# Sixteen modulation rows on TensorE as rows of PSUM instead of columns, in a two-block transformer kernel

## The reference, cut to what matters

```
c_act = silu(c)                                  # c: 1 x 1024
mod = c_act @ mod_w[l] + mod_b[l]                # 1 x 6144
sh1, sc1, g1, sh2, sc2, g2 = split(mod, 6)       # 1024 each
h = rmsnorm(x, norm_g[l, 0]) * (1 + sc1) + sh1
y = gla_mixer(h, ...)                            # gated linear attention
x = x + g1 * y
```

## Time and profile before

| | us |
|---|---|
| median of 3 runs | 2828.66 |
| lowest and highest of them | 2826.82, 2834.25 |
| profiled execution | 2830.2 |
| its span in the profile | 2828.1 |
| PE busy | 2742.2 (97%) |
| DVE busy | 2151.8 (76%) |
| ACT busy | 1324.3 (47%) |
| POOL busy | 1295.6 (46%) |

### The profile page before, as it was taken

The page is one execution under the profiler, slowest core; times in us unless marked ns, Lnnn a source line. Parts: engine busy times, 40 slices in busy tenths (PEclk is TensorE's granted clock), DMA queues, the critical chain, the costliest instruction groups (busy, mean ns, idle before and its releaser), DMA issues.

```text
span 2828.1 us, 53480 instructions
## 1 busy us (share of the span) xinstructions
PE 2742.2 (97%) x16662; PEld 2411.2 (85%) x16662; DVE 2151.8 (76%) x4127; ACT 1324.3 (47%) x2533; POOL 1295.6 (46%) x977
## 2 busy tenths in 40 slices
PE   6999999999999999899999999999999999999998
PEld 6688999999778877799999998777778989776666
DVE  7736996999888886758957898888867545467775
ACT  1115555333455555555564334555554633355553
POOL 4930897666444440006986664544420000244442
PEclk8999999999999999899999999999999999999999
DMA  7634555666666663144554566766635533389994
GB/s 257 214 115 134 183 181 194 203 204 207 236 238 233 229 227 115 42 159 149 184 173 141 174 202 211 260 222 230 223 141 170 177 131 122 111 327 359 356 356 167
DMA packets 179366, 562.52 MB, mean 199 GB/s; under 512 B 16288, under 2 KB 19104, under 8 KB 179120
## 3 DMA queue, kind: packets, MB, share of 16 engines
q1 hardware_dynamic: 176880, 556.86, 57.1%
q10 hardware_dynamic: 2368, 4.19, 0.4%
HBM read 559.94 MB, written 1.05 MB: 198 GB/s over the span
## 4 chain that ended last, share of the span: by engine, by line
PE 78%; PEld 6%; issue 6%; DVE 5%; POOL 2%; ACT 2%; DMA 1%; ACTq 0%; DVEq 0%; PEldq 0%; SPq 0%; POOLq 0%
PE bank L1113 22%; PE bank L1082 20%; PE bank L826 8%; PE bank L1406 7%; PEld bank L1082 6%; PE bank L1427 4%; PE bank L1062 4%; PE bank L885 4%; PE bank L850 1%; POOL arena L2902 1%; DVE h_parts L2435 1%; PE bank L771 1%; DVE a_parts L2438 1%; ACT arena L1702 1%; PE bank L1252 1%
## 5 line engine op out<-in xcount | busy, mean ns | idle before, releaser
L2848 POOL TENSOR_TENSOR w_parts<-ring,w_parts 128x512 fp32r<-128x512 f32 x512 | 667.2, 1310 | 511.5 <-ACT w_parts L1619 479.3
L1082 PE MATMUL bank<-h_parts,w_parts 128*128 128x256 f32 x6144 | 771.4, 285 | 4.4 <-POOL w_parts L2848 2.2
L1082 PEld LDWEIGHTS bank<-h_parts,w_parts 128*128 128x128 f32 x6144 | 747.5, 192 | 4.8 <-POOL w_parts L2848 2.4
L1619 ACT ACTIVATE w_parts<-ring 128x512 fp32r<-128x512 f32 x512 | 322.8, 631 | 436.3 <-PE bank L1082 435.8
L1113 PE MATMUL bank<-w_parts,a_parts 128*128 128x512 f32 x1536 | 370.3, 397 | 4.1 <-DVE a_parts L2438 4.1
L1113 PE MATMUL bank<-h_parts,a_parts 128*128 128x512 f32 x1536 | 365.7, 393 | 4.6 <-DVE a_parts L2438 4.4
L1113 PEld LDWEIGHTS bank<-h_parts,a_parts 128*128 128x128 f32 x1536 | 284.6, 188 | 79.1 <-DVE a_parts L2438 20.9
L1113 PEld LDWEIGHTS bank<-w_parts,a_parts 128*128 128x128 f32 x1536 | 286.0, 190 | 63.7 <-DVE a_parts L2438 5.1
L826 PE MATMUL bank<-h_parts,w_parts 128*128 128x256 f32 x2304 | 283.2, 285 | 4.0 <-DVE w_parts L2009 4.0
L826 PEld LDWEIGHTS bank<-h_parts,w_parts 128*128 128x128 f32 x2304 | 280.3, 193 | 5.1 <-issue 4.4
L1677 ACT ACTIVATE a_parts<-arena 128x256 fp32r (+1 forms) x256 | 107.0, 418 | 359.4 <-PE bank L1113 359.4
(11 more groups left out here) (397 smaller groups left out, 4318.1 us busy)
## 6 DMA issues: line engine op xcount, KB each, us to landing
ring<-stream SPq DMA_DIRECT2D x594, 512.0 KB, 3.3
arena<-stream SPq DMA_DIRECT2D x105, 1024.0 KB, 7.2
arena<-stream SPq DMA_DIRECT2D x144, 512.0 KB, 4.5
hT<-stream SPq DMA_DIRECT2D x96, 256.0 KB, 3.1
hT<-stream SPq DMA_DIRECT2D x32, 512.0 KB, 4.5
mean<-stream SPq DMA_DIRECT2D x32, 512.0 KB, 4.5
arena<-consts ACTq DMA_DIRECT2D x1, 1536.0 KB, 6.2
xT<-xin ACTq DMA_DIRECT2D x1, 1024.0 KB, 10.7
```

The source lines that it names most:

```text
L1082: mm = pe.matmul(bank[k][:, 0:T], w[:, wp, ws], h_parts[:, hp, 4 * j + q, :], start=(j == 0 and q == 0 and i == 0), stop=(j == 1 and q == ...
L1619: act.activation(w_parts[half % HALVES][:, 0, :], ring[slot_][:, j * 512:(j + 1) * 512], ACT.Copy).then_inc(sem(f"{n}_high"), 1)
L2848: pool.tensor_tensor(w[:, 1, :], ring[(base + k) % RING][:, j * 512:(j + 1) * 512], w[:, 0, :].bitcast(F32), ALU.subtract).then_inc(sem(f" ...
```

## The change

- Twelve rows are direct instead of seven, and DVE keeps four (2, 5, 8 and 11).
- In a direct row the operands change places. The column of `cact` is the stationary operand (128 x 1), the weights are the moving one (128 x 128), and eight matmuls add up in one row of PSUM: partition 0, 128 columns. Four rows share a bank; banks 4 and 5 are used in turn.
- ACT copies these rows from PSUM to partition 0 of a buffer in SBUF in four pieces (`first_rows_act`), and PE turns each row of 1 x 128 into a column of 128 x 1 by a matmul with a single one (`turned`): four behind the square sums, eight at the end. PE's rows 8 and 11 wait for earlier pieces to be copied.
- DVE's four rows no longer pass through the ring. Each has a buffer of its own into which it is loaded and in which it is multiplied.
- The ring holds 12 places for this stage instead of 16.
- The loads for POOL's rows 16 to 39 are issued later: the first behind place `gla` + 3 of the ring (whose load waits for the twelfth direct row), 18 in all spaced by four thirds of a place, and the last six behind `gla` + 27 as before.

```
-DIRECT_MODS = (0, 2, 4, 7, 9, 11, 13)
-SUMMED_MODS = tuple(m for m in range(FIRST_MODS) if m not in DIRECT_MODS)
+SUMMED_MODS = (2, 5, 8, 11)
+DIRECT_MODS = tuple(m for m in range(FIRST_MODS) if m not in SUMMED_MODS)
+N_DIRECT = len(DIRECT_MODS)
...
+        def first_row(i):
+            return G.v.rearrange("p a n -> p (a n)")[0:1, i * P:(i + 1) * P]
+        def first_bank(i):
+            return bank[(4, 5, 4)[i // 4] if i < 11 else 5]
...
-                if RING <= i < RING + FIRST_MODS:
-                    m = i - RING
-                    if m in DIRECT_MODS:
-                        sp.wait_ge(sem("first_direct"), DIRECT_MODS.index(m) + 1)
-                    else:
-                        sp.wait_ge(sem("first_product"), SUMMED_MODS.index(m) + 1)
+                if RING <= i < RING + N_DIRECT:
+                    sp.wait_ge(sem("first_direct"), i - RING + 1)
...
-            at = [8, 10, 14, gla + 1] + [gla + 2 + 3 * i // 2 for i in range(14)] + [gla + 27] * 6
-            loads_with_mods(0, MO["peer0_q"][1], MODS_GLA, MODS_GLA[0], at)
+            at = [gla + 3 + 4 * i // 3 for i in range(18)] + [gla + 27] * 6
+            for m in range(FIRST_MODS):
+                if m in SUMMED_MODS:
+                    i = SUMMED_MODS.index(m)
+                    sp.dma_start(first_buffer(i), stream[m]).then_inc(sem(f"first_landed{i}"), 16)
+                else:
+                    load(DIRECT_MODS.index(m))
+            loads_with_mods(N_DIRECT, MO["peer0_q"][1], MODS_GLA, MODS_GLA[0], at)
...
+            def turned(i):
+                m = DIRECT_MODS[i]
+                pe.matmul(t[:, m:m + 1], first_row(i), ones[0:1, 0:1], start=True, stop=True)
+            for i in range(N_DIRECT):
+                pe.wait_ge(landed_sem("mod", i), landed_at("mod", i))
+                if i == 8:
+                    pe.wait_ge(sem("first_evicted"), 1)
+                if i == 11:
+                    pe.wait_ge(sem("first_evicted"), 2)
+                w = slot("mod", i)
                 for q in range(DC):
-                    mm = pe.matmul(t[:, m:m + 1], w[:, q * P:(q + 1) * P], cact[:, q:q + 1], start=(q == 0), stop=(q == DC - 1))
+                    mm = pe.matmul(first_bank(i)[0:1, i % 4 * P:(i % 4 + 1) * P], cact[:, q:q + 1],
+                                   w[:, q * P:(q + 1) * P], start=(q == 0), stop=(q == DC - 1))
                 mm.then_inc(sem("first_direct"), 1)
-                if i == 2:
+                if i == 5:
                     pe.wait_ge(sem("loaded"), 16 * N_LOADS)
                     for c in range(DC):
                         square_sum_pe(pe, "0a", c)
+                    for j in range(4):
+                        if j == 0:
+                            pe.wait_ge(sem("first_evicted"), 1)
+                        turned(j)
             for i, m in enumerate(SUMMED_MODS):
                 pe.wait_ge(sem("first_made"), i + 1)
                 column(pe, t[:, m:m + 1], first_part(i))
+            for n, (lo, hi) in enumerate(((4, 8), (8, 11), (11, 12))):
+                pe.wait_ge(sem("first_evicted"), n + 2)
+                for j in range(lo, hi):
+                    turned(j)
...
+        def first_rows_act(act, lo, hi):
+            act.wait_ge(sem("first_direct"), hi)
+            act.activation(first_rows(lo, hi), first_bank(lo)[0:1, lo % 4 * P:(lo % 4 + hi - lo) * P],
+                           ACT.Copy).then_inc(sem("first_evicted"), 1)
...
             squares_act(act, "0a")
+            first_rows_act(act, 0, 4)
             root_act(act, "0a", rs[:, :])
+            first_rows_act(act, 4, 8)
+            first_rows_act(act, 8, 11)
+            first_rows_act(act, 11, 12)
             shift_act(act, "0a", mod(0))
```

More of the change, by code:

```diff
@@ L137 @@
 SO, _ = offsets(STREAM)
-MO, N_MAIN = offsets([(name, FIRST_MODS if name == "mod" else n) for name, n in STREAM
+MO, N_MAIN = offsets([(name, N_DIRECT if name == "mod" else n) for name, n in STREAM
                       if not name.endswith("_v") or not name.startswith("peer")])
@@ L382, in block_program @@
         G.o = ph(8 * T).rearrange("p (c t) -> p c t", c=8)
+        G.landing = ph(2 * CH)
         ph = Place(ROUTE_TILE * T)
@@ L535, in main_row @@
         def main_row(i):
-            return i + (40 - FIRST_MODS if i >= FIRST_MODS else 0) + sum(V_ROWS for at in after_v if i >= at)
+            if i < N_DIRECT:
+                return DIRECT_MODS[i]
+            return i + 40 - N_DIRECT + sum(V_ROWS for at in after_v if i >= at)
         def mod_buffers(seg):
@@ L554, in first_buffer, with first_rows @@
         def first_buffer(i):
-            return arena[:, 5 * CH + (i % 2) * CH:5 * CH + (i % 2 + 1) * CH]
+            return arena[:, (5 + i) * CH:(6 + i) * CH] if i < 2 else G.landing[:, (i - 2) * CH:(i - 1) * CH]
+        def first_row(i):
+            return G.v.rearrange("p a n -> p (a n)")[0:1, i * P:(i + 1) * P]
+        def first_bank(i):
+            return bank[(4, 5, 4)[i // 4] if i < 11 else 5]
+        def first_rows(lo, hi):
+            return G.v.rearrange("p a n -> p (a n)")[0:1, lo * P:hi * P]
         def first_part(i):
@@ L926, in mod_pe @@
         def mod_pe(pe):
-            pe.sem_inc(ring_free, RING + FIRST_MODS)
+            pe.sem_inc(ring_free, RING + N_DIRECT)
             for b in range(4):
@@ L933, in mod_pe @@
             pe.wait_ge(sem("cact"), 1)
-            for i, m in enumerate(DIRECT_MODS):
-                pe.wait_ge(landed_sem("mod", m), landed_at("mod", m))
-                w = slot("mod", m)
+            def turned(i):
[8 more added lines that the diff above has]
+                w = slot("mod", i)
                 for q in range(DC):
-                    mm = pe.matmul(t[:, m:m + 1], w[:, q * P:(q + 1) * P], cact[:, q:q + 1], start=(q == 0), stop=(q == DC - 1))
+                    mm = pe.matmul(first_bank(i)[0:1, i % 4 * P:(i % 4 + 1) * P], cact[:, q:q + 1],
+                                   w[:, q * P:(q + 1) * P], start=(q == 0), stop=(q == DC - 1))
                 mm.then_inc(sem("first_direct"), 1)
-                if i == 2:
+                if i == 5:
                     pe.wait_ge(sem("loaded"), 16 * N_LOADS)
@@ L2041, in first_mods_dve @@
             for i in which:
-                m = SUMMED_MODS[i]
                 buf = first_buffer(i)
-                dve.wait_ge(landed_sem("mod", m), landed_at("mod", m))
-                dve.tensor_tensor(buf.rearrange("p (k n) -> p k n", k=DC), slot("mod", m)[:, :].rearrange("p (k n) -> p k n", k=DC),
-                                  c_b, ALU.mult).then_inc(sem("first_product"), 1)
+                b3 = buf.rearrange("p (k n) -> p k n", k=DC)
+                dve.wait_ge(sem(f"first_landed{i}"), 16)
+                dve.tensor_tensor(b3, b3, c_b, ALU.mult).then_inc(sem("first_product"), 1)
                 dve.wait_ge(sem("first_product"), i + 1)
@@ L2933, in _ @@
             cact_dve(dve)
-            first_mods_dve(dve, range(5))
+            first_mods_dve(dve, range(3))
             dve.wait_ge(sem("loaded"), 16 * N_LOADS)
             norm_root_dve(dve, "0a")
-            first_mods_dve(dve, range(5, len(SUMMED_MODS)))
+            first_mods_dve(dve, range(3, len(SUMMED_MODS)))
             mod_dve(dve)
```

## The result

The changed kernel takes 2835.63 us in the median of 12 runs (2826.76 to 2842.58), the kernel before 2828.57 us on the same chip (12 runs, 2824.76 to 2834.25): a ratio of 1.0021, interval 1.0011 to 1.0031. The forecast was 2825.6 with a small gain; it is slower by 7.1 us. The profiled execution took 2838.96 us, its span is 2837.0.

A forecast was written before the change was run, and what follows sets the result against it. DVE's nine rows bound the first norm's chain, but POOL's rows close the stage at 177 us; 2830.2 profiled - 3.1 for POOL's earlier end = 2827.1, less 1.5 for the median: 2825.6; range 2815 to 2839, the forecast's own 2820 to 2829.

The forecast's parts named there:

- Pitch and clock of the new rows: Twelve direct rows, first stage: 116 ns a matmul, 1.85 us a row, clock rising at 11.9, twelfth done at 36.3.
- First projection: Its first matmul starts at 40.9 us instead of 52.73, 11.8 us earlier.
- The clock held from there to the first q projection: PE stands under 2 us, so the clock stays up, saving 2.0 us more; first query projection at 44.4.
- POOL's end: POOL's rows 16 to 39 start at 41.2 us and end at 174.6 against 177.67, 3.1 us earlier.
- The ring: Ring loads stand behind SP's wait for POOL to finish a row: about 4.5 us of PE idle time.
- POOL is the limit, PE about 9 us ahead: Before the output projection PE idles some 9 us, waiting for POOL's last row.
- The failed step: PE's losses before the output projection fit in some 9 us of slack; a wait there costs nothing new.
- The rivals: Four alternatives: POOL not the end (0.15), clock staying low (0.14), 160 ns pitch (0.07), late direct-row loads (0.07).
- the second: Clock doesn't rise with one weight column in the direct rows; twelfth ends about 52, time about 2839; chance 0.14.

The follow-up runs named there:

- experiment 5: Changed kernel with DVE's two gate scalings moved behind the first step's state copies: 2831.6 us, ratio 1.0009.
- experiment 4: Changed kernel with six unneeded 128x256 matmuls added in the recurrence, two in each of three steps: 2831.31 us, ratio 1.0007.
- experiment 7: Changed kernel with POOL's product for rows 16 to 39 made over the first eighth of its columns only: 2815.88 us, ratio 0.9951.
- experiment 3: Changed kernel with its twelve direct rows in the old form, weights stationary and one moving column: 2850.7 us, ratio 1.0073.
- experiment 10: Changed kernel with POOL's first four loads early again, gate scalings behind the first states, and later POOL loads closer together: 2815.48 us, ratio 0.9957.
- experiment 6: Kernel before with two more DVE scalings by 1.0 behind the two gate scalings: 2849.55 us, ratio 1.0077.
- experiment 2: Kernel before, old rows kept, with only the changed kernel's list of POOL load places: 2837.12 us, ratio 1.002.

## Why the prediction was wrong, step by step

- **Pitch and clock of the new rows: right.** 111 ns (116 taken), and the clock rose at about 12 us with one weight column: 6, 10 and 11 instructions in the microseconds from 11, 12 and 13. The twelfth row ended at 36.5 (36.3).
- **First projection: right.** 41.27 (40.9).
- **The clock held from there to the first q projection: wrong, small.** The granted clock fell to 0.50 at 39.5 and was back at 46.3. It fell while PE was still at work on the turning and the closing columns, 26 narrow instructions from 36.4 on, and not in a gap, which was all that I had looked for; the next ring load was issued at 47.9 instead of 44.4.
- **POOL's end: mis-sized by 3 us.** Rows 126.7 us (134.7 from start to end less 8.0 of waits; 126.5 forecast). Its start was at 42.94 (41.2), since the first load took 6.05 us to land and not 4.5, and the waits were 8.0 us (6.9), for the late q load. So 177.65 instead of 174.6: no gain.
- **The ring: right.** 2.13 + 2.08 us of idle time before the output projection (4.5).
- **POOL is the limit, PE about 9 us ahead: right as long as the clock holds.** 8.07 us in experiment 5.
- **The failed step:** that what PE loses on its way is "all inside PE's slack of some 9 us", with the ring's 4.5 us as the only loss counted, and that "the clock at the output projection was at the lower level before too …, so a wait there costs nothing new". I looked at the clock at both ends of the mixer, not in its middle, where it stood at 1.00 from 150 to 175 and was there to be lost; and the one gap that I measured a fall by was the 5 us of the earlier trace rows. I moved DVE's work and POOL's rows against each other by some 7 us and priced their contention as a total only, never for the few instructions that PE stands behind. The runs put in its place: 1.5 us more for two scalings, 0.88 us of waiting, then half rate, 12.2 us in all, so that the output projection started 6.7 us later than before. Cures for the wait or the gap that leave the loads late (experiments 4 and 5) give back 4 us of the 7 and bring the median to where no difference can be told. The last words failed even for the wait that I had forecast: in experiment 5 it costs the columns behind it 1.6 us.
- **The rivals.** None had it. The time came near the second's 2839, but by another mechanism.

What is shown and what isn't: waits of 0.88, 1.12, 1.28 and 3.23 us in the recurrence went with a fall that lasted to its end; with 0.20 us and with none the clock held, but for the 3.4 us of experiment 7. One wait was made on purpose in the kernel before, and there the clock fell while PE stood. Which length decides can't be read from these cases, and why the clock fell without a wait in experiment 7 stays open. That the spread of the changed kernel's runs (its two fastest, 2826.8 and 2827.3, have the highest mean clock, 0.985, against 0.979 to 0.983) comes from runs in which the fall stayed out fits, but only the profiled runs have a trace.

## What to carry to other kernels

When loads of a side engine are moved, look up which of its instructions will then lie beside the ones that TensorE waits for, and not only when the side engine ends. A slack of TensorE is not free to spend: look for stretches of narrow matmuls at 1.00 in the granted clock, since here 0.88 us of waiting in front of them went with a loss of 12.2 us. And a lead in a stage that another engine closes is worth nothing until that engine is fed without gaps; with it fed, the same rows brought 10 us at the output projection.

## What the runs showed of the hardware

- The clock came back neither in 24 us of 128x64 and 64x256 matmuls in which PE was never idle (windows 155:175 above) nor in 20.6 us of matmuls with one moving column (experiment 3, by their 215 ns; the column of the granted clock reads 1.00 there); it did in the 128x256 ones that followed each. The Trainium skill ("TensorE: Matmul & The Clock Gate", section "Why this matters for your kernels") advises to keep TensorE busy continuously for the highest matmul throughput; in both of these stretches it was, and it worked at the lower level. The same 128x64 and 64x256 matmuls that didn't raise the clock in these traces kept it at 1.00 in the kernel before.
- The clock also fell while PE was busy: at 39.5 in the kernel after, at 136.2 in experiment 7 and at 162.5 in experiment 10, each time in or up to 1.3 us behind 128x1 columns.
- Two DVE TENSOR_SCALARs of 128x1024 took 1.87 us beside POOL's small additions and 3.94 beside its 128x1024 product and first addition, in one run (experiment 6). POOL's product went from 1.90 to 2.34 there and its first addition from 1.27 to 1.59; in experiment 2 the product kept its 1.90 beside such scalings. The Trainium skill ("GPSIMD Engine Reference", section "1. Specifications") names contention of GpSimd with DVE instructions in a perf mode with two ports or with two inputs in SBUF. The trace agrees that there is some, and shows that it depends on which of POOL's instructions lies beside; whether the scalings, which have one tensor as input, ran in such a mode no run here shows.
- A load that SP issued at 36.89, as the last of a burst, took 6.05 us to be used, against 4.5 in the median of such loads.
